# First gather of a mixture-of-experts stage: its table made from the tokens' place numbers as they stand, first rows copied in quarters, one prefetched part held until the gather is issued

## The reference, cut to what matters

```python
hn = rms_norm(x, norm_ffn)
x = x + hier_moe(hn, ...)
# hier_moe: g_idx = argmax of 4 group logits; top 2 of the 8 experts in that group
for gi in range(N_GROUPS):
    h = silu(einsum('td,edf->tef', xt, w_gate[gi])) * einsum('td,edf->tef', xt, w_up[gi])
    out = out + einsum('tef,efd->td', h * combine[:, gi, :, None], w_down[gi])
```

## Time and profile before

| what | us |
|---|---|
| median of 3 runs | 605.76 |
| lowest and highest | 605.17, 606.72 |
| the profiled execution, its own time | 605.26 |
| its span | 603.5 |
| PE busy | 577.0 |
| DVE busy | 260.3 |
| ACT busy | 215.0 |
| POOL busy | 60.3 |

### The profile page before, as it was taken

How to read it: one execution, slowest core, us unless ns; L and a number is a source line. 1 busy time by engine, 2 the same in 40 slices (tenths; PEclk the granted TensorE clock), 3 DMA queues, 4 the chain that set the end, 5 groups by cost and what they waited for, 6 DMA issues and landing times.

```text
span 603.5 us, 8714 instructions
## 1 busy us (share of the span) xinstructions
PE 577.0 (96%) x3442; PEld 437.3 (72%) x3445; DVE 260.3 (43%) x584; ACT 215.0 (36%) x437; POOL 60.3 (10%) x104
## 2 busy tenths in 40 slices
PE   7999999999999999999999998999999999887795
PEld 4978989888788888888888874766666666543452
DVE  4646677645445765533472375212111211103255
ACT  6634566555786522422152241011111111111114
POOL 3110000001000001100000012012211121112001
PEclk9999999999999999999999999999999999999999
DMA  8365130712231222197789677999999999999995
GB/s 296 92 205 177 59 111 5 287 62 71 71 104 46 61 70 71 38 344 280 287 315 406 248 259 273 389 414 423 424 421 423 424 427 419 424 425 424 424 421 208
DMA packets 59291, 155.78 MB, mean 258 GB/s; under 512 B 8284, under 2 KB 38388, under 8 KB 47600
## 3 DMA queue, kind: packets, MB, share of 16 engines
q1 hardware_dynamic: 54512, 145.74, 63.2%
q0 software_dynamic: 4720, 9.45, 4.1%
q10 hardware_dynamic: 16, 0.00, 0.0%
HBM read 147.31 MB, written 15.75 MB: 270 GB/s over the span
## 4 chain that ended last, share of the span: by engine, by line
PE 79%; DMA 11%; DVE 3%; SPq 3%; ACT 1%; issue 1%; POOL 1%; DVEq 0%; POOLq 0%; ACTq 0%
PE mid_rows L810 17%; PE last_rows L810 16%; PE bank L1247 12%; DMA slot2b<-expert_w_up 9%; PE bank L810 7%; PE bank L803 5%; PE mid_rows L1267 5%; SPq L554 3%; PE bank L1321 2%; PE mid_rows L945 2%; PE last_rows L868 2%; PE mid_rows L1340 1%; DMA w<-w_in 1%; PE bank L1347 1%; PE mid_rows L868 1%; PE bank L923 1%
## 5 line engine op out<-in xcount | busy, mean ns | idle before, releaser
L1247 PE MATMUL bank<-slots,xgT 128*64 128x256 f32 x544 | 73.0, 381 | 4.5 <-DMA slot2b<-expert_w_up 1.9
L1910 DVE TENSOR_TENSOR w_low<-w,w_high 128x1024 fp32r<-128x1024 f32 x32 | 39.2, 1225 | 78.6 <-ACT w_high L1524 78.6
L1247 PEld LDWEIGHTS bank<-slots,xgT 128*64 128x64 f32 x544 | 49.2, 137 | 22.2 <-issue 4.0
L1524 ACT ACTIVATE w_high<-w 128x1024 fp32r<-128x1024 f32 x32 | 33.7, 1054 | 48.6 <-PE last_rows L810 48.6
L2265 DVE TENSOR_SCALAR y<-mid_rows,slot_weights 128x512 f32<-128x512 f32 x14 | 10.5, 751 | 88.4 <-PE mid_rows L1267 88.4
L1699 ACT ACTIVATE y<-mid_rows,slot_weights 128x512 f32<-128x512 f32 x14 | 9.6, 687 | 84.5 <-PE mid_rows L1267 56.4
L1247 PE MATMUL bank<-slot2b,xgT 128*64 128x256 f32 x208 | 32.9, 381 | 0.0
L1267 PE MATMUL mid_rows<-slots,hT 128*64 128x512 f32 x112 | 29.1, 594 | 2.7 <-issue 2.7
L1693 ACT ACTIVATE h_silu<-bank 128x256 f32<-128x256 f32 x14 | 5.4, 384 | 66.3 <-PE bank L1247 66.3
L810 PE MATMUL mid_rows<-x_high,w_high 128*128 128x512 f32 x72 | 28.7, 399 | 0.0
L810 PE MATMUL mid_rows<-x_high,w_low 128*128 128x512 f32 x72 | 28.2, 391 | 0.0
(11 more groups left out here) (430 smaller groups left out, 1391.5 us busy)
## 6 DMA issues: line engine op xcount, KB each, us to landing
slots<-expert_w_up SPq DMA_DIRECT2D x18, 1024.0 KB, 23.9
slots<-expert_w_gate SPq DMA_DIRECT2D x17, 1024.0 KB, 12.4
slots<-expert_w_down SPq DMA_DIRECT2D x15, 1024.0 KB, 23.9
slot2b<-expert_w_gate SPq DMA_DIRECT2D x9, 1024.0 KB, 16.9
w<-w_in SPq DMA_DIRECT2D x16, 512.0 KB, 3.6
slot2b<-expert_w_up SPq DMA_DIRECT2D x8, 1024.0 KB, 27.5
slot2a<-expert_w_down SPq DMA_DIRECT2D x6, 1024.0 KB, 21.4
w<-w_in SPq DMA_DIRECT2D x7, 840.0 KB, 4.5
```

The costliest lines, as they stand in the source:

```text
L1247: ins = mm(bank[2][e * SLOTS:(e + 1) * SLOTS, m * FE:(m + 1) * FE], xgT[:, c, e * SLOTS:(e + 1) * SLOTS], weights(own, m, e, c * FE, (c + ...
L1524: A(wh2[:, u % 2, :], raw2[:, u % 2, :], ACT.Copy).then_inc(s["hi_done"], 1)
L1910: V.tensor_tensor(wl2[:, u % 2, :], raw2[:, u % 2, :], wh2[:, u % 2, :].bitcast(F32), ALU.subtract).then_inc(s["lo_done"], 1)
```

## The change

- PE's first table has two columns only and is made from `place` itself. `hot` compares `place` with `first_slots`, a row of the numbers that the slots of pair 0 have (2^23 plus slot, plus 448 more for the second expert), so no cutting of the number comes before it. `by_pair[:, :, 0:2]` holds the plain token numbers for it. Only column 0 of `ztab` and `gtab` is made, and the first gather is issued from it.
- The full table of 16 columns is made as before, behind that, into columns 1 to 15. The copy to `dealt` moves there too. The second gather waits for it (`gcolm_done` 2). Semaphore counts behind are renumbered.
- The rows of the first pair are turned into four banks by two chunks each for the first three quarters' banks and the second half of bank 4 (`turn_first`), and copied out in quarters, ACT and DVE in turn (`first_x`). The first gate product waits for each quarter.
- `router_in(1)` moves from DVE to ACT: the copy of the second half of the second 128 rows.
- The filler matmuls are 20, 5, 8 and 5 for 22, 11 and 17.
- SP waits before part 20 for `pool_step` 1, which POOL now raises behind the first gather.

```diff
             sp.wait_ge(s["hT_done"], 2 * NT)
+            sp.wait_ge(s["pool_step"], 1)
             load_part(20)
...
             pool.wait_ge(s["gcolm_done"], 1)
             first_gather(0)
+            pool.sem_inc(s["pool_step"], 1)
             pool.wait_ge(s["xt_done"], 2)
+            pool.wait_ge(s["gcolm_done"], 2)
             first_gather(1)
...
             def route(t0, t1):
-                pe.wait_ge(s["hnT_outA"], t1)
-                pe.wait_ge(s["hnT_outD"], t1)
+                pe.wait_ge(s["hnT_outA"], t1 + 1)
+                pe.wait_ge(s["hnT_outD"], t1 - 1)
...
-            keep_busy(22)
+            keep_busy(20)
...
-            keep_busy(11)
+            keep_busy(5)
 
             pe.wait_ge(s["rl_out"], 2)
             for k in range(2 * NT):
                 pe.wait_ge(s["hot_done"], k + 1)
+                ins = mm(bank[3][:, TABLE][:, 0:2], hot[:, k, :], by_pair[:, k, 0:2], start=(k == 0),
+                         stop=(k == 2 * NT - 1), skip_group_check=True)
+            ins.then_inc(s["first_done"], 1)
+            keep_busy(8)
+            for k in range(2 * NT):
+                pe.wait_ge(s["hot_done"], 2 * NT + k + 1)
                 ins = mm(bank[3][:, TABLE][:, 0:PAIRS], hot[:, k, :], by_pair[:, k, :], start=(k == 0), stop=(k == 2 * NT - 1),
                          skip_group_check=True)
             ins.then_inc(s["first_done"], 1)
-            keep_busy(17)
+            keep_busy(5)
...
+            def turn_first():
+                pe.wait_ge(s["gathered0"], 16)
+                xv = xg[0].rearrange("p (q c) -> p c q", c=KC)
+                for c in range(KC):
+                    at = bank[(0, 1, 5, 4)[c // 2]][:, (c % 2 + (2 if c >= 6 else 0)) * P:]
+                    ins = tr(at[:, 0:P], xv[:, c, :])
+                    if c == 1:
+                        ins.then_inc(s["first_done"], 1)
+                    if c % 4 == 3:
+                        ins.then_inc(s["xt_done"], 1)
...
             turned_rows(1)
+            act.wait_ge(s["hT_done"], 4)
+            A(hnT[:, 4:8, P:2 * P], bank[TURNED[1][1]][:, :].rearrange("p (c n) -> p c n", c=4), ACT.Copy).then_inc(s["hnT_outA"], 1)
...
+            def first_x():
+                act.wait_ge(s["first_done"], 3)
+                A(xgT[:, 0:2, :], bank[0][:, 0:2 * P].rearrange("p (c n) -> p c n", c=2), ACT.Copy).then_inc(s["xgt_outA"], 1)
+                act.wait_ge(s["xt_done"], 2)
+                A(xgT[:, 4:6, :], bank[5][:, 0:2 * P].rearrange("p (c n) -> p c n", c=2), ACT.Copy).then_inc(s["xgt_outA"], 1)
...
             router_in(0)
-            router_in(1)
             normed(3)
...
-            V.tensor_copy(dealt.rearrange("p (x e l) -> p x e l", l=4, e=8),
-                          K["iota"].rearrange("p (x l e) -> p x e l", l=4, e=8))
+            for e in range(2):
+                V.tensor_scalar(first_slots[:, e * SLOTS:(e + 1) * SLOTS].rearrange("p (x e l) -> p x e l", l=4, e=8),
+                                K["iota"][:, e * SLOTS:(e + 1) * SLOTS].rearrange("p (x l e) -> p x e l", l=4, e=8),
+                                UNIT + e * (SEQ - SLOTS), None, ALU.add)
+            V.tensor_copy(by_pair[:, :, 0:2], bc(K["tokval"], 2))
...
             link(V.tensor_reduce(place[:].rearrange("p (k t) -> p k t", k=2), sel[:], AX, ALU.add))
+
+            for w in range(2):
+                ks = slice(w * NT, (w + 1) * NT)
+                V.tensor_tensor(hot[:, ks, :], first_slots.unsqueeze(1).to_broadcast([P, NT, P]), bc(place[:, ks], P),
+                                ALU.is_equal).then_inc(s["hot_done"], NT)
...
+            dve.wait_ge(s["first_done"], 1)
+            link(V.tensor_scalar(ztab[:, 0:1], bank[3][:, TABLE][:, 0:1], float(NOWHERE), None, ALU.add))
+            V.tensor_scalar(gtab[:, 0:1], ztab[:, 0:1], 1, None, ALU.logical_shift_right).then_inc(s["gcolm_done"], 1)
...
+            link(V.tensor_copy(dealt.rearrange("p (x e l) -> p x e l", l=4, e=8),
+                               K["iota"].rearrange("p (x l e) -> p x e l", l=4, e=8)))
             dve.wait_ge(s["wo_done"], 2 * NT)
...
-            dve.wait_ge(s["first_done"], 1)
-            link(V.tensor_scalar(ztab[:, 0:PAIRS], bank[3][:, TABLE][:, 0:PAIRS], float(NOWHERE), None, ALU.add))
-            V.tensor_scalar(gtab[:, 0:PAIRS], ztab[:, 0:PAIRS], 1, None, ALU.logical_shift_right).then_inc(s["gcolm_done"], 1)
+            dve.wait_ge(s["first_done"], 2)
+            link(V.tensor_scalar(ztab[:, 1:PAIRS], bank[3][:, TABLE][:, 1:PAIRS], float(NOWHERE), None, ALU.add))
+            V.tensor_scalar(gtab[:, 1:PAIRS], ztab[:, 1:PAIRS], 1, None, ALU.logical_shift_right).then_inc(s["gcolm_done"], 1)
```

More of the change, by code:

```diff
@@ L303, in hybrid_encoder @@
         y_sb = place_at(D, "y", D)[:, :]
+        first_slots = place_at(0, "first_slots", P)[:, :]
         h_silu, h_sb = place_at(SMALL, "h_silu", FE)[:, :], place_at(SMALL + FE, "h_sb", FE)[:, :]
@@ L730, in gather @@
                 nc.gpsimd.tensor_copy(gcolm[:, k:k + 1], gtab[:, bass.ds(t, 1)]).then_inc(s["gcolm_done"], 1)
-                pool.wait_ge(s["gcolm_done"], n)
+                pool.wait_ge(s["gcolm_done"], n + 1)
                 pool.sem_inc(s["pool_step"], 1)
@@ L1147, in turn_hn @@
                 for c in range(KC):
-                    if t == NT - 1 and c % 4 == 0:
-                        pe.wait_ge(s["hnT_outD"], 2 + c // 4)
+                    if t == NT - 1 and c == 0:
+                        pe.wait_ge(s["hnT_outA"], 3)
+                    if t == NT - 1 and c == 4:
+                        pe.wait_ge(s["hnT_outD"], 2)
                     ins = tr(bank[TURNED[t][c // 4]][:, (c % 4) * P:(c % 4 + 1) * P], hn_st[:, t, c * P:(c + 1) * P])
@@ L1207, in _ @@
             ins.then_inc(s["first_done"], 1)
-            keep_busy(17)
+            keep_busy(5)
             def slot_weights():
                 pe.wait_ge(s["hTs_done"], 1)
-                pe.wait_ge(s["hot_done"], 2 * NT + 1)
+                pe.wait_ge(s["hot_done"], 4 * NT + 1)
                 for k in range(2 * NT):
@@ L1218, in later_tables @@
             def later_tables():
-                pe.wait_ge(s["hot_done"], 6 * NT + 1)
+                pe.wait_ge(s["hot_done"], 8 * NT + 1)
                 for k in range(2 * NT):
@@ L1223, in later_tables @@
                 ins_.then_inc(s["first_done"], 1)
-                pe.wait_ge(s["hot_done"], 8 * NT + 1)
+                pe.wait_ge(s["hot_done"], 10 * NT + 1)
                 for k in range(2 * NT):
@@ L1241, in gate_or_up @@
                 for c in range(KC):
[L1242 to L1245, removed]
+                    if m == 0 and c % 2 == 0 and halved:
+                        pe.wait_ge(s[("xgt_outA", "xgt_outD")[c // 2 % 2]], c // 4 + 1)
+                    if m == 0 and c == 0 and not halved:
+                        pe.wait_ge(s["xgt_outA"], n + 2)
+                    if m == 0 and c == KC // 2 and not halved:
+                        pe.wait_ge(s["xgt_outD"], n + 2)
                     for e in range(2):
@@ L1272, in weights_of @@
                 return n, n % 4, lambda m: arrived[n, m]
-            turn_x(0, 0, 1)
+            turn_first()
             gate_or_up(0, 0, *weights_of(0), halved=True)
@@ L1710, in _ @@
             act.sem_inc(s["y_outA"], 1)
-            x_evac(0)
+            first_x()
             for n in range(LAST):
@@ L2237, in later_tables @@
                                     ALU.is_equal, ALU.mult).then_inc(s["hot_done"], 1)
-                dve.wait_ge(s["first_done"], 2)
+                dve.wait_ge(s["first_done"], 4)
                 V.tensor_scalar(ztab[:, later], bank[3][:, TABLE][:, later], float(NOWHERE), None, ALU.add).then_inc(s["tabs_done"], 1)
@@ L2247, in later_tables, with first_x @@
                 dve.wait_ge(s["ws_out"], 2)
+            def first_x():
+                dve.wait_ge(s["xt_done"], 1)
+                V.tensor_copy(xgT[:, 2:4, :], bank[1][:, 0:2 * P].rearrange("p (c n) -> p c n", c=2)).then_inc(s["xgt_outD"], 1)
+                dve.wait_ge(s["xt_done"], 2)
+                V.tensor_copy(xgT[:, 6:8, :], bank[4][:, 2 * P:].rearrange("p (c n) -> p c n", c=2)).then_inc(s["xgt_outD"], 1)
             def x_evac(n):
```

## The result

| | median, us | runs |
|---|---|---|
| before | 605.16 | 20 |
| changed | 606.68 | 20 |

The ratio is 1.0023 with a 95% interval of 1.0015 to 1.003: the change made the kernel slower by 1.4 us (0.9 to 1.8). The forecast was 1.1 us faster, with a range up to 606.3. The sign was wrong, and the time lies outside the range. The profiled execution took 607.59 us (span 605.8), 2.3 more than the one before (605.26).

A forecast was written before the change was run, and what follows sets the result against it. The weight stream through the DMA engines was taken to bound the end. PE comes 1.62 + 0.5 = 2.1 us earlier, 1.0 is given back by the hold, leaving 1.08: 604.7 us from 605.76, 8 in 10 range 603.2 to 606.3.

The forecast's parts named there:

- What bounds the kernel: Second half: the end is set by when the last experts' weights are through the DMA engines; a PE tail follows.
- The table 1.62 us earlier: Before the first gather: 1.32 us from the shorter table chain plus 0.30 upstream, so the gather starts at 369.07.
- The 0.30 us for the router's copy and the fillers: Upstream of the table: 0.15 us from moving the copy to ACT, some 0.15 from two fewer fillers; bounds 0 and 0.4.
- DVE's new work and the page on the shared port: Around the table: new DVE work hidden, 0.1 to 0.2 us if late; the 0.27 us copy could hold the gather.
- The held part: Part 20 behind the gather: issued at 370.32, part 22 flows at 374.27; 1.0 us of the gain is given back.
- the late end, since the engine works in order: POOL's signal for part 20 was taken to come at the end of the gather's instruction, 1.19 us later, at 370.26.
- rival A: Part 20's signal is early and harmless: part 20 out at about 368.3, gain up to 2.1 us, 603.7; chance 0.22.
- the sum: From the gather to the weight stream: part 22 starts at 374.27 for 375.35, 1.08 us earlier, forecasting 604.7 us.
- Rival B: The gather meets part 20 and takes 5.3 us to land, at 374.4; nothing gained, 605.8; chance 0.14.
- The granted clock is 1.00 in all these stretches, so it takes no part: PE's clock in the stretches around the first gather: read as 1.00 before, so given no effect on time.
- Quarters: First rows copied in quarters: transposes to first gate product 0.99 us for 1.49, so 0.5 us earlier against the landing.

The follow-up runs named there:

- e1: The changed kernel with 14 filler matmuls for 5 ahead of the first transposes, nothing else: 604.93 us, 0.9998 of the kernel before.
- e11: The changed kernel without the wait ahead of part 20, with router_in(1) back on DVE and 22 fillers: 603.53 us, 0.9976 of the kernel before.
- e12: The changed kernel without the wait ahead of part 20, with 6, 8 and 3 fillers added around pairs 10 to 14: 607.52 us, 1.003 of the kernel before.
- e2: The changed kernel without SP's wait on pool_step ahead of part 20: 603.54 us, 0.9976 of the kernel before.
- e3: The changed kernel with part 20's signal raised by a small POOL memset behind the gather's descriptors: 604.18 us, 0.9978 of the kernel before.
- e6: The changed kernel with part 20's signal from a POOL memset behind the gather's descriptors, and 9 fillers for 5: 603.6 us, 0.998 of the kernel before.
- e7: The kernel before with 5 fillers for 17 ahead of the first transposes, nothing else: 607.58 us, 1.0035 of the kernel before.
- e10: The changed kernel without the wait ahead of part 20, its first rows copied in halves as before: 604.35 us, 0.9984 of the kernel before.
- e8: The changed kernel, part 20 not held, 8 fillers, part 22 sent on a late POOL signal instead of the landing: 603.79 us, 0.9979 of the kernel before.
- e5: The changed kernel without the wait ahead of part 20 and with 8 fillers for 5: 603.88 us, 0.9983 of the kernel before.
- e9: The kernel before with part 20 held for POOL's signal and 29 fillers for 17: 608.68 us, 1.0066 of the kernel before.
- e4: The kernel before with only the hold added, part 20 waiting for POOL's signal behind the first gather: 609.61 us, 1.0061 of the kernel before.

## Why the prediction was wrong

- *What bounds the kernel:* right. The changed kernel and e1 to e11 follow the bytes moved by 390 us: each one's profiled time lies within 1.1 us of that account (GB/s less 313, times 90 us, over 422 GB/s). e12 is 4.8 us off it; its fillers stand in the late stretch, which the account doesn't cover.
- *The table 1.62 us earlier:* the table's part is right. From the end of the place reduction to the gather's start it took 4.6 us before (366.08 to 370.69) and 3.3 after (365.82 to 369.15), 1.3 less as forecast. The 0.30 us for the router's copy and the fillers can't be told from the shift between executions, and e11 shows no gain from them. Nor was the table's part of e2's 1.4 us measured by itself.
- *DVE's new work and the page on the shared port:* no effect. The copy of the dealt slots took 0.27 us again and ended at 368.97, ahead of the gather, and from POOL's queue to the gather's start it was 0.78 us as before. The gather's descriptors took 1.21 us beside the 1.29 us of the comparisons, against 1.19 before. The rule on fp32 copies in the Trainium skill, page "SBUF — State Buffer", section "SBUF: two separate sides", wasn't put to the test, for the two didn't meet.
- *The held part: this step failed.* The prediction took "the late end, since the engine works in order", and let part 20 go out at 370.32. It went out at 369.02. POOL's queue runs ahead of its engine: the `sem_inc` stood at 368.92, 0.23 us before the instruction that it follows in the program. The 0.78 us between queue and start had been named as a sign of this under rival A, and given less weight than it deserved. With the signal really late e3 gives the forecast's instants and its gain (1.3 us, forecast 1.1), and e6 the same gain within the intervals.
- *What the early signal does:* rival A had the early signal, but not its harm: the sum took part 20 to cost the landing at most 0.4 us, and it cost 1.3 to 1.9. Rival B's landing of 5.3 us (chance 0.14) came as 5.24. It was taken from a gather beside the stream of weights, not from one met by a single part, so that the number fits so well is in part luck.
- *"The granted clock is 1.00 in all these stretches, so it takes no part": this sentence failed too, and it is about half of the loss.* It read the clock of the kernel before as a property of the place. The clock was held there by 17 fillers, which the change cuts to 5. For the late landing alone rival B forecast no change against the kernel before, and e1 shows just that (0.9998). The clock adds 1.5 us (e1 against the changed kernel), and e7 shows 2.1 for the same cut in the kernel before. The prediction counted the fillers only as something in the way.
- *Quarters:* the gate product comes 0.4 us earlier against the landing (1.09 us behind the first transpose in e1 and e2, where the sum had 0.99). The sum gave that no worth in time, for it took part 22's start as the only point that binds. e10 puts it at 0.5 us, not clear of the noise. But the halves of parts 23 and 24, which PE's first gate product releases, bind as well: that is how the clock costs time in e7, with part 22 out on time, and why e8's earlier part 22 gains nothing.

So the loss splits, by ratios and with a plus for slower: table and quarters -1.4 (e2), hold +1.3 (e1 against e2), clock +1.5 (the changed kernel against e1), together +1.4. The three add up by construction, each being the step from one kernel to the next, so their sum proves nothing; the second is the least sure, for the intervals of e1 and e2 overlap a little, and with e5 or e6 in e2's place it is 0.9 to 1.1. That the signal's place makes the gather late is shown by e2 and e3, that the fallen clock costs time by e1 and e7. Where the gather lands early, more fillers than five bring nothing that can be told (e5 against e2). Open: the excess of e9, why the hold costs more in the kernel before than in the changed one, and what makes the long executions (605 to 607) of the faster kernels. Not shown either: whether a fall of the clock near 560 us makes them; e12 didn't tell, and e2's profiled execution had such a fall (0.66 at 555 to 560) at 603.18 us, one of its shortest.

The version that beats both is the changed kernel less one line (e2): 603.54 us, 0.9976 (0.9962 to 0.999) of the kernel before.

## What to carry to other kernels

Here a semaphore that POOL's queue raised behind its indirect DMA came 0.23 us ahead of that DMA's start, and one raised by a small instruction of the engine came behind its descriptors. To order another transfer behind it, let an instruction of the engine raise it, and check in the timeline which of the two goes out first. When a change moves the end of a wait, size the fillers for the new wait, and for the latest landing, not for the hoped one; a clock of 1.00 in the profile before is what the old fillers bought. And where a stream is full to the end, compare the bytes moved by a fixed time; for the edits made ahead of the stream that one number gave the profiled time within 1.1 us.

## What was not expected of the hardware

- Part 20, 0.13 us ahead of a gather, put its landing at 5.24 us after its start, where landings with no part held took 3.34 to 3.88; the part alone is 2.48 us at 422 GB/s (the prediction's figure). A part 1.4 us behind the gather's start cost nothing that can be seen. The Trainium skill, page "DMA: Bandwidth & Descriptors", section "Queues, rings and completion order", has each DMA engine take turns between its queues packet by packet; these landings don't contradict it, but no run here looks at single packets, so how the part delays the gather isn't shown.
- The clock isn't told by the length of the idle time alone. It fell at idle times of 2.16 (changed), 2.90 (e4), 3.61 (e7), 0.71 (e3) and 0.80 us (e12), and held through 1.16 in the kernel before (17 fillers ahead), 0.57 (e2) and 0.59 (e10). In e4 PE had stood since 372.87 and the clock was 1.00 until after 375.0; in the changed kernel PE stood since 372.27 and it was 0.50 by 373.5. Once fallen it stayed at 0.50 through 3.0 (e4) to 5.2 us (changed kernel) of PE's work.
